# Two attentions of a two-block transformer kernel: the softmax weights' reciprocal scaling is moved from VectorE to ScalarE

## The reference, cut to what matters

```python
def a_block(q, t0):      # 4 heads, each with two score maps c = 0, 1
    logits = einsum('bqhcd,bkhcd->bhcqk', q, ka) * scale
    p = softmax(where(causal, logits, -inf))
    attn = p[:, :, 0] - lam * p[:, :, 1]
    return einsum('bhqk,bkhe->bqhe', attn, va)

def b_block(q, qidx, widx, t0):   # 8 heads, keys chosen by an index score
    isc = einsum('bqhk,bqh->bqk', relu(einsum('bqhd,bkd->bqhk', qidx, ki)), widx)
    _, idx = top_k(isc, k_sel)    # k_sel = 128
    p = softmax(logits over the chosen keys)
    return einsum('bhqk,bqkhd->bqhd', p, v_g)
```

## Time and profile before

| | |
|---|---|
| runs of the kernel | 3640.53, 3639.43, 3628.37 us; median 3639.43 |
| the profiled execution | 3628.36 us, its span (first to last instruction) 3627.1 us |
| PE busy | 3536.8 us of the span, mean granted clock 0.981 |
| DVE busy | 1901.2 us |
| ACT busy | 1232.4 us |
| POOL busy | 501.6 us |

### The profile page before, as it was taken

How to read it: one execution, slowest core, us unless ns; L and a number is a source line. 1 busy time by engine, 2 the same in 40 slices (tenths; PEclk the granted TensorE clock), 3 DMA queues, 4 the chain that set the end, 5 groups by cost and what they waited for, 6 DMA issues and landing times.

```text
span 3627.1 us, 41473 instructions
## 1 busy us (share of the span) xinstructions
PE 3536.8 (98%) x16908; PEld 2864.9 (79%) x16908; DVE 1901.2 (52%) x3317; ACT 1232.4 (34%) x1657; POOL 501.6 (14%) x438
## 2 busy tenths in 40 slices
PE   8999999999999999999999999988999999999999
PEld 5888877788888888877788887645888888888887
DVE  5555743664556445644652345696553434564433
ACT  3222472442224222562442234334442223342221
POOL 1010220110012000221210011111111111201111
PEclk9999999999999999999999999978999999999999
DMA  6444311134442344211132222100212222212221
GB/s 267 177 166 176 108 58 48 47 129 150 163 143 110 142 163 155 90 53 41 68 135 98 93 68 80 67 1 26 103 69 95 93 103 98 105 70 93 95 103 70
DMA packets 53041, 373.45 MB, mean 103 GB/s; under 512 B 5874, under 2 KB 6002, under 8 KB 10099
## 3 DMA queue, kind: packets, MB, share of 16 engines
q1 hardware_dynamic: 52850, 370.79, 28.3%
HBM read 368.67 MB, written 2.10 MB: 102 GB/s over the span
## 4 chain that ended last, share of the span: by engine, by line
PE 44%; DVE 4%; ACT 1%; issue 1%; POOL 0%; DVEq 0%; ACTq 0%; POOLq 0%
PE ps L1450 44%; PE ps L1470 0%; DVE s_tmp L2369 0%; ACT s_tmp L1945 0%; DVE s_tmp L2528 0%; ACT s_wh L1795 0%; DVE s_sm L2508 0%; DVE s_tmp L2541 0%; DVE s_hl L2103 0%; DVE s_tmp L2359 0%; DVE s_sm L2367 0%; DVE s_xr L2239 0%; DVE s_bm L2510 0%; DVE s_sm L2347 0%; DVE s_tmp L2545 0%
## 5 line engine op out<-in xcount | busy, mean ns | idle before, releaser
L1450 PE MATMUL ps<-s_hh,s_wh 128*128 128x512 f32 x2552 | 1012.7, 397 | 17.8 <-POOL s_hl L2665 13.0
L1450 PE MATMUL ps<-s_hh,s_wl 128*128 128x512 f32 x2552 | 997.6, 391 | 0.0
L1450 PE MATMUL ps<-s_hl,s_wh 128*128 128x512 f32 x2552 | 997.1, 391 | 0.0
L2110 DVE TENSOR_TENSOR s_wl<-s_stage,s_wh 128x2048 fp32r<-128x2048 f32 (+1 forms) x276 | 623.9, 2260 | 652.9 <-ACT s_wh L1795 652.7
L1795 ACT ACTIVATE s_wh<-s_stage 128x2048 fp32r<-128x2048 f32 (+1 forms) x276 | 519.1, 1881 | 585.0 <-PE ps L1450 431.6
L1450 PEld LDWEIGHTS ps<-s_hh,s_wh 128*128 128x128 f32 x2552 | 480.8, 188 | 139.8 <-issue 36.6
L1450 PE MATMUL ps<-s_ah,s_wh 128*128 128x512 f32 x1408 | 561.8, 399 | 0.2 <-DVE s_wl L2110 0.2
L1450 PEld LDWEIGHTS ps<-s_hh,s_wl 128*128 128x128 f32 x2552 | 480.7, 188 | 102.5
L1450 PEld LDWEIGHTS ps<-s_hl,s_wh 128*128 128x128 f32 x2552 | 481.3, 189 | 98.4 <-issue 1.7
L1450 PE MATMUL ps<-s_ah,s_wl 128*128 128x512 f32 x1408 | 549.9, 391 | 0.0
L1450 PE MATMUL ps<-s_al,s_wh 128*128 128x512 f32 x1408 | 549.3, 390 | 0.0
(11 more groups left out here) (442 smaller groups left out, 3754.6 us busy)
## 6 DMA issues: line engine op xcount, KB each, us to landing
s_stage<-in_w_ada SPq DMA_DIRECT2D x64, 1024.0 KB, 4.8
s_stage<-in_ffn_w_gate SPq DMA_DIRECT2D x44, 1024.0 KB, 4.8
s_stage<-in_ffn_w_up SPq DMA_DIRECT2D x44, 1024.0 KB, 4.8
s_stage<-in_ffn_down SPq DMA_DIRECT2D x32, 1024.0 KB, 4.8
s_stage<-in_w_up SPq DMA_DIRECT2D x32, 1024.0 KB, 4.8
s_stage<-in_down_m SPq DMA_DIRECT2D x32, 1024.0 KB, 4.7
s_stage<-in_w_in SPq DMA_DIRECT2D x24, 1024.0 KB, 4.8
s_stage<-in_ffn_down SPq DMA_DIRECT2D x16, 768.0 KB, 4.2
```

Source lines behind the costliest of these rows:

```text
L1450: return pe.matmul(out, lhs, rhs, start=start, stop=stop, skip_group_check=True)
L2110: ins = dve.tensor_tensor(m.wl(ws)[:, a:z], m.STAGE[:, j % NS, a:z], m.wh(ws)[:, a:z].bitcast(F32), ALU.subtract)
```

## The change

For kind "b", DVE keeps the reciprocal, and the scaling by it becomes an ACT instruction (`Copy` with a per-partition scale, in place, fp32). In `ea_mix` DVE no longer scales the first map. It makes c = (1/sum1) * lambda * sum0 with one small instruction, adds map1 * c to the unscaled map 0, and ACT then scales the sum by 1/sum0. The events `at.n` (kind "b") and `ea.mix`, for which PE's transposes and the reuse of buffers wait, are now ACT's.

```diff
 (scalar)
+    def at_norm(u, n, q, sm):
+        if u[0] == "b":
+            e.wait_ge(("at.rc", u))
+            act.activation(m.tmp(q)[:, 0:n], m.tmp(q)[:, 0:n], ACT.Copy, scale=m.small(sm)[:, 3:4]).then_inc(
+                *e.up("act_scale", "at.n", u))
+
+    def ea_mix(h, i, q, s):
+        a = m.tmp(q[0])[:, 0:(i + 1) * P]
+        e.wait_ge(("ea.add", h, i))
+        act.activation(a, a, ACT.Copy, scale=m.small(s[0])[:, 3:4]).then_inc(*e.up("act_scale", "ea.mix", h, i))
 (vector, at_norm)
         dve.reciprocal(rc, total).then_inc(*e.up("dve_at", "at.rc", u))
-        e.wait_ge(("at.rc", u))
-        dve.tensor_scalar(a, a, rc, None, ALU.mult).then_inc(*e.up("dve_at", "at.n", u))
+        if u[0] != "b":
+            e.wait_ge(("at.rc", u))
+            dve.tensor_scalar(a, a, rc, None, ALU.mult).then_inc(*e.up("dve_at", "at.n", u))
 (vector, ea_mix)
         dve.reciprocal(s1[:, 3:4], s1[:, 2:3]).then_inc(*e.up("dve_ea", "ea.rc", h, i, 1))
-        e.wait_ge(("ea.rc", h, i, 0))
-        dve.tensor_scalar(a0, a0, s0[:, 3:4], None, ALU.mult).then_inc(*e.up("dve_ea", "ea.p0", h, i))
         e.wait_ge(("ea.rc", h, i, 1))
-        dve.tensor_tensor(s1[:, 4:5], s1[:, 3:4], m.LAM[:, 0:1], ALU.mult).then_inc(*e.up("dve_ea", "ea.l", h, i))
-        e.wait_ge(("ea.p0", h, i), ("ea.l", h, i))
-        dve.scalar_tensor_tensor(a0, a1, s1[:, 4:5], a0, ALU.mult, ALU.add).then_inc(*e.up("dve_ea", "ea.mix", h, i))
+        dve.scalar_tensor_tensor(s1[:, 4:5], s1[:, 3:4], m.LAM[:, 0:1], s0[:, 2:3], ALU.mult, ALU.mult).then_inc(
+            *e.up("dve_ea", "ea.l", h, i))
+        e.wait_ge(("ea.l", h, i))
+        dve.scalar_tensor_tensor(a0, a1, s1[:, 4:5], a0, ALU.mult, ALU.add).then_inc(*e.up("dve_ea", "ea.add", h, i))
```

More of the change, by code:

```diff
@@ L2061, in scalar @@
         ret_av=ret_av, ret_sub=ret_sub, m_part=m_part, at_score=at_score, at_turn=at_turn, at_av=at_av, pos_sin=pos_sin,
-        lam=lam, e_copy=e_copy, e_sq=e_sq, e_tcopy=e_tcopy, ix_score=ix_score, ea_score=ea_score, ea_turn=ea_turn,
+        lam=lam, e_copy=e_copy, e_sq=e_sq, e_tcopy=e_tcopy, ix_score=ix_score, at_norm=at_norm, ea_mix=ea_mix, ea_score=ea_score, ea_turn=ea_turn,
         ea_av=ea_av, ck_part=ck_part, e_vb=e_vb, an_sq=an_sq, an_out=an_out, o_wp=o_wp, po_mean=po_mean,
```

## The result

Before: 3636.36 us, median of 16 runs (3628.36 to 3642.79). After: 3645.37 us, median of 16 runs (3639.26 to 3651.30). The ratio is 1.0025, 95% interval [1.0017, 1.0033]: 9 us slower, inside the 0.5% that was called no change, and inside the range of 3620 to 3655. I had forecast plus 2 and 3641; the size of the loss was missed by 7 us, and plus 9 lies just outside the minus 6 to plus 8 to which I had given 0.50.

The account below looks back on a forecast made before the run. PE bounds the whole; in the changed mixer DVE (2370 to 2440), half-clock PE (2440 to 2471), then engines' mutual waiting. Terms -1.6 + 0 - 0.3 + 4 = plus 2 us: 3641 on the median, range 3620 to 3655.

Parts of the forecast that it names:

- The kind of work moved: Sign that the change happened: L2541 gone, L2369 down to 64 instructions, 48 new ACT rows of 0.40 to 0.72 us.
- Rival 3: The change does not do what it says: an activation table load between Exp and Copy; slower, chance 0.01.
- 2471 to 2520, plus 4: Thirteen pairs: ACT's exps and older copies precede the scaling, so PE's transposes come later; plus 4 us.
- minus 5 and plus 14.6: Ends for 2471 to 2520: DVE's relief counts 13 times 0.4, or all 26 ACT scalings fall into the path.
- near twice: Sign in the pairs: PE's wait for the scaling near twice 11.5 us, naming ACT.
- 2370 to 2440, minus 1.6: Eleven mixes, DVE the bound at 92%: minus 2.6 us of DVE, plus 1 for PE's lateness; ends minus 6.9, plus 2.
- 2440 to 2471, minus 0.3: Six units, 2.12 us of DVE, PE at half clock the bound: minus 0.3 us, ends minus 2 and plus 1.
- 2320 to 2370, zero: Five mixes, 1.83 us of DVE covered by PE's products: zero; without that cover, 5 times 0.35 us later.
- The clock: PE keeping full clock 2410 to 2470: minus 24 us, chance 0.05; half clock in 2471 to 2520: plus 25, 0.08.
- rival 2: ACT becomes the bound in 2471 to 2520: plus 10 us, 3649, chance 0.15; with half clock plus 25, 3664, 0.08.
- the last transposes later than 2525: Sign from the last pair's transposes: between 2518 and 2525 for the forecast, later for ACT as the bound.

## Why the prediction was right or wrong

- **The kind of work moved: right.** L2541 is gone and 48 ACT rows are there. By size they take, as priced, 0.40, 0.51, 0.61 and 0.72 us:

```profile
L1944 ACT ACTIVATE s_tmp<-s_tmp,s_sm x26: 385/506/717, 2458.2 to 2530.8; 128x128 f32<-128x128 f32 x7, 128x256 f32<-128x256 f32 x7, 128x384 f32<-128x384 f32 x7, 128x512 f32<-128x512 f32 x5
...
L1950 ACT ACTIVATE s_tmp<-s_tmp,s_sm x15: 401/511/723, 2330.9 to 2447.4; 128x128 f32<-128x128 f32 x4, 128x256 f32<-128x256 f32 x4, 128x512 f32<-128x512 f32 x4, 128x384 f32<-128x384 f32 x3
```

(the view of one line: min, median and max ns). DVE's product with three inputs takes 0.22, not 0.15 us, but the addition starts 0.25 after it, as priced (0.26): nothing hangs on it. Rival 3 is out. (26 and 15 of the rows are shown; the other 6 and 1 write to `s_xe`.)

- **2471 to 2520, plus 4: right in mechanism, perhaps too small in size.** Alone it measured 6.2 with an interval of about 3 us to either side, which takes in the 4. ACT's order, the later transposes (3.1 us from the exp of A, for 3.2) and the wait that names ACT are all there; PE's wait grew 1.4 times, not "near twice". The bounds, minus 5 and plus 14.6, can now be named: with the work gone from both engines it is minus 8.5, which is more than the 13 times 0.4 that I gave DVE's relief as its end, and the two together say that the scalings cost nearly what they would if they lay whole in the path (15 us for the 18 us that 32 of them take).

- **2370 to 2440, minus 1.6: wrong by its premise, small.** "DVE at 92%: it is the bound" led me to count every us that DVE is spared. Without any ACT scaling the stretch between the sixth and the last addition had 1.6 us less of DVE and was 0.1 us shorter. A busy share of 92% over 70 us was still not an unbroken chain: DVE idled for what it was spared. In the earlier trace rows PE's waits for the addition remain after as waits for the scaling (5.2 us in five, between the sixth and the last addition, both before and after).

- **2440 to 2471, minus 0.3.** No experiment has this stretch by itself; it is part of the third piece above.

- **2320 to 2370, zero: the step that failed.** I wrote that "the products cover it", with ends of minus 1 and plus 1, and "with that cover gone it is 5 times 0.35 later". The cover is 44.8 us of 50, and I asked nothing about the 5 us that are left. Half of them are one wait of 2.51 us, in which PE has run out of products and the chain to the next one leads through ACT: eviction of q, square, two copies, and DVE's low part. That chain was in the trace of before. I had even named what is queued behind the new wait, "copies for which there is room with ACT at 32%", and asked for room where I should have asked for the order: ACT was idle, but it was idle at the head of its queue, waiting for the addition, with the copies behind it. The price was 1.2 us at one place and, in three of four profiles, over 4 more of half clock, not five times 0.35. The kernel with this one unit changed shows the place: plus 5 (interval plus 1 to plus 10), and without it the two-map part costs nothing.

- **The clock.** I had considered it for 2410 to 2470 in both directions. Over these microseconds it is 0.67 after and 0.56 before, but the work has moved against them; between the sixth and the last addition it is 0.76 for 0.80, and from there to the last reciprocal 0.78 for 0.77. It fell where I had not looked, after the one wait that grew.

- **The rivals.** The size (plus 9) is that of rival 2 (plus 10), and so is my sign for it, the last transposes later than 2525 (they start at 2531.56). The reason is not: ACT is busy for 34.8 us of 49 in that stretch, not full, and 5.8 of the 12.6 us by which the last reciprocal is late were lost before 2377. The longer instructions as such (48 times 0.2 us) give near 10 by accident. By my own rows it would have been 48 times 0.12, as the 48 scalings took 21.2 us on DVE and I had them at 0.56 each on ACT; and fifteen of the sixteen two-map scalings cost nothing while one costs 5 us. The page "ScalarE: Activation LUTs" of the Trainium skill, section Rules for kernel authors, sends a plain multiplication to VectorE for its cost per element; at 512 columns it took 0.49 us there and 0.72 on ACT, and the change lost, so both agree in direction, but the loss does not go by these lengths.

- **The number.** Landing in the range was partly luck. Two of the terms were off: minus 1.6 for 2370 to 2440, where nothing was gained, and zero for 2320 to 2370, where one unit alone cost 5. And the median of the kernel before came out 3 us lower over 16 runs than over the three that I had, which took back part of the miss in 3641.

What stays open: the parts measured alone (10 and 6) are more than the whole (9 and 12 in two sets of runs), and one unit is worth 3 to 13 us by the differences of the medians, depending on which pair of kernels one takes. Where in the mixer the half clock falls differs between executions of one kernel, and its total there (61 to 92 us in the thirteen profiles) moves the time by as much as these differences. No run held the clock fixed, so its share in the 9 us is known only by the estimate above.

## What to carry to other kernels

When a wait is added to an engine, don't ask how busy the engine is: list what stands behind the waiting instruction in its queue, and follow each of these to the engine that sets the pace. The place to look is where that engine already has its longest idle time, even in a stretch where it is 90% busy. And a saving on a busy engine is worth what an experiment without the work says, here 8.5 us in one stretch and nothing in another with a busier DVE.

## What the runs showed that was not expected

- One wait of PE that grew from 2.5 to 3.7 us was followed, in three of four profiles, by some 12 us of half clock under unbroken matmuls: 48 to 50 of them in 14 us, against 77 before and 83 where there was no half clock. Where it came, it cost over 4 us, more than three times the growth of the wait itself. The mean clocks of the runs with and without that one scaling (0.9767 against 0.9801 and 0.9794) say that it was no accident of a few profiles.
- The same program, with the same wait, ran those 14 us at a granted clock of 0.57 in one execution and 1.00 in another. The Trainium skill says in "TensorE: Matmul & The Clock Gate", section Why this matters for your kernels, that idle gaps between bursts of matmuls lose the full clock. Behind the wait of 3.7 us three of four profiles agree and the fourth doesn't; behind the wait of 2.5 us seven of nine show half clock, two of them 10 us of it.
- 21 us of instructions taken off one engine and given to another that was two thirds idle made the kernel 9 us slower. DVE's busy time fell by only 13.4 us for it.
